# Moving the loop over overflow blocks of a mixture-of-experts layer from the end to behind the fifth step

## The reference, cut to what matters

```python
def run_block(args):
    toks, gts, ei = args
    xb = hf[toks]
    hb = jax.nn.silu(xb @ w1[ei]) * (xb @ w3[ei])      # 1024 -> 512
    return (hb @ w2[ei]) * gts[:, None]                # 512 -> 1024

ys = lax.map(run_block, (row_tok.reshape(-1, R), row_gate.reshape(-1, R), block_e))
return jax.ops.segment_sum(ys.reshape(P, D), row_tok, num_segments=T)
```

## Time and profile before

| what | value |
|---|---|
| median of 3 runs | 1550.96 us (1550.81 to 1551.97) |
| profiled execution | 1557.21 us |
| its span | 1555.1 us |
| PE busy | 1360.8 us (88%) |
| DVE busy | 605.8 us (39%) |
| ACT busy | 407.4 us (26%) |
| POOL busy | 82.0 us (5%) |
| DMA traffic | 326.68 MB, mean 210 GB/s |

### The profile page before, as it was taken

The page is one execution under the profiler, slowest core; times in us unless marked ns, Lnnn a source line. Parts: engine busy times, 40 slices in busy tenths (PEclk is TensorE's granted clock), DMA queues, the critical chain, the costliest instruction groups (busy, mean ns, idle before and its releaser), DMA issues.

```text
span 1555.1 us, 17299 instructions
## 1 busy us (share of the span) xinstructions
PE 1360.8 (88%) x6335; PEld 685.4 (44%) x6335; DVE 605.8 (39%) x1370; ACT 407.4 (26%) x894; POOL 82.0 (5%) x113
## 2 busy tenths in 40 slices
PE   4999999999997889988899927999999899899750
PEld 3644444555654444444455524444433343343320
DVE  2535457400345666666333363222222232222206
ACT  4243311114665655555133310000000000000005
POOL 0000000010003000000000001000000000000004
PEclk9999999999997999999999956999999999999885
DMA  9714135220006940000633354999999999999929
GB/s 338 156 41 142 67 118 213 83 80 0 1 1 159 278 165 1 0 1 0 262 118 109 121 202 145 385 394 406 393 402 400 416 397 400 407 397 411 403 83 306
DMA packets 109451, 326.68 MB, mean 210 GB/s; under 512 B 26796, under 2 KB 51000, under 8 KB 100792
## 3 DMA queue, kind: packets, MB, share of 16 engines
q1 hardware_dynamic: 96296, 295.67, 50.8%
q0 software_dynamic: 6288, 18.90, 3.8%
q10 hardware_dynamic: 6784, 11.02, 1.9%
HBM read 285.69 MB, written 42.49 MB: 211 GB/s over the span
## 4 chain that ended last, share of the span: by engine, by line
PE 31%; SPq 12%; DMA 8%; DVE 5%; issue 2%; ACT 2%; POOL 1%; ACTq 0%; DVEq 0%; POOLq 0%
SPq L652 9%; DMA arena<-expert_w 7%; PE ps L1472 7%; PE ps L1512 6%; PE ps L1562 4%; PE ps L1523 4%; PE ps L1378 2%; PE ps L1395 2%; PE ps L1415 2%; SPq L650 1%; ACT arena L1040 1%; POOL arena L840 1%; PE ps L1502 1%; SPq L699 1%; PE ps L1457 1%
## 5 line engine op out<-in xcount | busy, mean ns | idle before, releaser
L1231 PE MATMUL ps<-arena 128*128 128x512 f32 x512 | 222.0, 593 | 0.0
L1523 PE MATMUL ps<-arena 128*32 128x256 f32 (+1 forms) x1408 | 196.9, 498 | 26.4 <-DMA arena<-expert_w 24.1
L1562 PE MATMUL ps<-arena 128*32 128x256 f32 (+2 forms) x832 | 156.0, 509 | 4.7 <-issue 2.0
L1231 PEld LDWEIGHTS ps<-arena 128*128 128x128 f32 x512 | 96.6, 190 | 117.8 <-issue 117.7
L1242 PE MATMUL ps<-arena 128*128 128x512 f32 (+1 forms) x384 | 144.5, 535 | 1.4 <-DVE arena L1658 1.4
L1523 PEld LDWEIGHTS ps<-arena 128*32 128x32 f32 (+1 forms) x1408 | 73.6, 126 | 135.6 <-issue 118.4
L1512 PE MATMUL ps<-arena 128*128 128x512 f32 x256 | 117.8, 619 | 6.0 <-DVE arena L2069 6.0
L1472 PE MATMUL ps<-arena 128*128 128x512 f32 x256 | 112.7, 592 | 0.1
L1040 ACT ACTIVATE arena<-arena 128x640 f32<-128x640 f32 (+7 forms) x128 | 92.8, 726 | 61.3 <-DVE arena L1871 61.3
L1242 PEld LDWEIGHTS ps<-arena 128*128 128x128 f32 x384 | 72.8, 192 | 66.2 <-issue 57.3
L1395 PE MATMUL ps<-arena 128*128 128x128 f32 x528 | 80.5, 286 | 21.2 <-ACT arena L1040 9.2
(11 more groups left out here) (326 smaller groups left out, 1309.2 us busy)
## 6 DMA issues: line engine op xcount, KB each, us to landing
arena<-expert_w SPq DMA_DIRECT2D x99, 2048.0 KB, 33.9
arena<-ada_w SPq DMA_DIRECT2D x12, 2048.0 KB, 9.3
d_y<-arena SPq DMA_DIRECT2D x24, 512.0 KB, 6.4
arena<-x SPq DMA_DIRECT2D x16, 512.0 KB, 4.4
arena<-w_in SPq DMA_DIRECT2D x4, 2048.0 KB, 11.0
d_y<-arena ACTq DMA_DIRECT2D x40, 128.0 KB, 8.2
arena<-w_out SPq DMA_DIRECT2D x2, 2048.0 KB, 14.1
out<-arena SPq DMA_DIRECT2D x8, 512.0 KB, 2.6
```

The costliest lines, as they stand in the source:

```text
L1231: last = nc.tensor.matmul(b, w(k), hT[:, k, 512 * c:512 * c + 512], start=(k == 0), stop=(k == KT - 1))
L1523: last = nc.tensor.matmul(ps[width * j:width * j + width, 2 if width == 64 else 3, 0:span], xgT[s][:, k, lo:lo + width], w_up[slots[n]][:, ...
L1562: last = nc.tensor.matmul(dst, hid_T[s][:, at_:at_ + width], w_down[slot][:, k, span * j:span * j + span], start=(k == 0), stop=(k == 3))
```

## The change

The loop over overflow blocks stands behind step 4, in front of step 5. It has 4 rounds, each with six nested conditions and six blocks. It has its own semaphores (`over_...`), counted from 1, with one unit given by GpSimd at the start so that block 0 waits for nothing of its own. All blocks use the same buffers (`xg[0]`, `xgT[0]`, `act1[0]`, `hid_e[0]`, `yo[0]`) and the same three slots, 3, 4 and 1. In `USES` the three matrices of the overflow blocks stand as a step numbered 32 behind step 4, so the loads of steps 5 and later take other slots than before, and three of them (w2 of step 6, w1 and w3 of step 8) wait for the slots of the overflow block, which are free when VectorE has left the loop (`over_end`).

On TensorE, down of step 4 is done before the loop and no longer between the turn of step 6 and the turn of step 5's hidden rows. VectorE waits before the loop until step 4's result has been stored. GpSimd issues the gather of step 6 only after `over_end`, and TensorE goes on with step 5 after `over_end`.

```diff
+OVER_AT, OVER, PER = 4, NE, 6
 def weight_uses():
     uses = []
     for q in range(NE):
-        uses += [(1, q), (3, q)] + [(2, q - 1)] * (q > 0)
+        uses += [(1, q), (3, q)] + [(2, q - 1)] * (q > 0 and q != OVER_AT + 1)
+        if q == OVER_AT:
+            uses += [(2, q)] + [(n, OVER) for n in (1, 3, 2)]
     return uses + [(2, NE - 1)]
...
             for v in range(NS - 1, len(LOADS)):
                 n, q = LOADS[v]
+                if q == OVER and n == 1:
+                    for j in range(3):
+                        slot_free(USES[v + j - NS])
+                    sp_blocks = sp.value_load(block_tab[0:1, 28:29], min_val=NE, max_val=NB)
+                    with sp.Fori(0, (NB - NE) // PER) as i, ExitStack() as rest:
+                        for s in range(PER):
+                            rest.enter_context(sp.If(PER * i + NE + s < sp_blocks))
+                            load_over(i, s)
+                if q == OVER:
+                    continue
                 place = ORDER[q]
...
             for q in range(NE):
                 gather_rows(q)
+                if q == OVER_AT + 1:
+                    pool.wait_ge(xg_turned, OVER_AT + 1)
...
+                    pool.wait_ge(over_end, 1)
...
+            def over_block(i, s):                      # PE
+                b = PER * i + s
+                pe.wait_ge(over_xg_in, 16 * b + 16)
+                pe.wait_ge(over_xgT, b + 1)
+                for k in range(KT):
+                    last = nc.tensor.transpose(turned_at(k, P), xg[so][:, k::KT], ident)
...
             for q in range(NE):
                 static_up(q)
                 if q + 1 < NE:
                     f_turn(q + 1, (q + 1) % 2, STEP_ROWS[q + 1], (q + 1) // 2 + 1)
-                if q:
+                if q and q != OVER_AT + 1:
                     static_down(q - 1)
                 f_turn_hidden(q, q % 2, STEP_ROWS[q])
+                if q == OVER_AT:
+                    static_down(q)
+                    pe.wait_ge(xgT_ready, OVER_AT + 2)
+                    pe.wait_ge(yo_ready, OVER_AT + 1)
...
+                    pe.wait_ge(over_end, 1)
...
+                if q == OVER_AT:                       # DVE
+                    static_result(q)
+                    dve.wait_ge(y_stored[so], STORES[OVER_AT + 2])
+                    v_blocks = dve.value_load(block_tab[0:1, 28:29], min_val=NE, max_val=NB)
+                    with dve.Fori(0, (NB - NE) // PER) as i, ExitStack() as rest:
+                        for s in range(PER):
+                            rest.enter_context(dve.If(PER * i + NE + s < v_blocks))
+                            over_block(i, s)
+                    dve.drain().then_inc(over_end, 1)
```

More of the change, by code:

```diff
@@ L100 @@
     SLOT_OF[u] = v if v < NS else SLOT_OF[USES[v - NS]]
-    fills[SLOT_OF[u]] += 1
+    fills[SLOT_OF[u]] += u[1] != OVER
     FILLS[u] = 16 * fills[SLOT_OF[u]]
-OVER_SLOT = [[SLOT_OF[USES[len(LOADS) - NS + 3 * s + j]] for j in range(3)] for s in range(2)]
-OVER_FILLS = [[16 * fills[j] for j in slots] for slots in OVER_SLOT]
+OVER_SLOT = [SLOT_OF[(n, OVER)] for n in (1, 3, 2)]
 STORES = [0, 0]
@@ L408, in build @@
         out_turned, outs_read = sem("out_turned"), sem("outs_read")
-        wout_scaled, pool_e, router_in, xt_in = sem("wout_scaled"), sem("pool_e"), sem("router_in"), [sem(f"xt_in{i}") for i in range(2)]
+        wout_scaled = sem("wout_scaled")
         diag_ready = sem("diag_ready")
@@ L424, in build @@
         table_ready = sem("table_ready")
-        mod_out, mod_in = sem("mod_out"), sem("mod_in")
+        mod_hop = sem("mod_hop")
         stage_f, y_zeroed = sem("stage_f"), sem("y_zeroed")
-        idx_seen, store_seen = sem("idx_seen"), sem("store_seen")
+        idx_seen = sem("idx_seen")
+        over_w_in = [sem(f"over_w_in{j}") for j in range(3)]
+        over_xg_in, over_silu, over_hid, over_hid_turned, over_hidT, over_stored = (
+            sem("over_" + n) for n in ("xg_in", "silu", "hid", "hid_turned", "hidT", "stored"))
+        over_free = [sem("over_" + n) for n in ("turned", "xgT", "up_half", "up", "down", "yo", "yo_free")]
+        over_turned, over_xgT, over_up_half, over_up, over_down, over_yo, over_yo_free = over_free
+        over_end, over_landed = sem("over_end"), sem("over_landed")
+        so = OVER_AT % 2
         y_in = [sem(f"y_in{i}") for i in range(NT)]
@@ L661, in slot_free @@
                 n, q = use
-                if n == 1:
+                if q == OVER:
+                    sp.wait_ge(over_end, 1)
+                elif n == 1:
                     sp.wait_ge(up_half, q + 1)
@@ L874, in _ @@
                 b = ready(act, ("adam", i))
-                nc.scalar.copy(ada_sum[0][:, i, :], b).then_inc(ada_copied, 1)
-                act.wait_ge(ada_copied, i + 1)
-                act.sem_inc(bank_read[JOB[("adam", i)] % 8], 1)
+                read(nc.scalar.copy(ada_sum[0][:, i, :], b), ("adam", i))
             act.wait_ge(mod_ready, 1)
@@ L1125, in store @@
                                .then_inc(y_stored[s], 16)
+            def over_block(i, s):
+                b = PER * i + s
+                act.wait_ge(over_up_half, b + 2)
+                nc.scalar.activation(act1[so], ps[:, 2, :], ACT.Silu).then_inc(over_silu, 1)
+                act.wait_ge(over_yo, b + 2)
+                act.sem_inc(idx_seen, 1)
+                to = d_y[bass.ds(P * (b + NE), P), :]
+                for n in range(2):
+                    act.dma_start(to[64 * n:64 * n + 64, :], yo[so][64 * n:64 * n + 64, :]).then_inc(over_stored, 16)
+                act.wait_ge(over_stored, 32 * b + 32)
+                act.sem_inc(over_yo_free, 1)
@@ L1143, in _ @@
[L1143 to L1146, removed]
+                if q == OVER_AT:
+                    store(q, q % 2, STEP_ROWS[q], ORDER[q])
+                    act.wait_ge(table_ready, 1)
+                    a_blocks = act.value_load(block_tab[0:1, 28:29], min_val=NE, max_val=NB)
+                    with act.Fori(0, (NB - NE) // PER) as i, ExitStack() as rest:
+                        for s in range(PER):
+                            rest.enter_context(act.If(PER * i + NE + s < a_blocks))
+                            over_block(i, s)
+                    act.drain().then_inc(over_landed, 1)
@@ L1147, in _ @@
+            store(NE - 1, 1, STEP_ROWS[NE - 1], ORDER[NE - 1])
+            for s in range(2):
+                act.wait_ge(y_stored[s], STORES[NE + s])
+                act.sem_inc(idx_seen, 1)
             act.drain().then_inc(stage_f, 1)
@@ L1584, in _ @@
                     f_turn(q + 1, (q + 1) % 2, STEP_ROWS[q + 1], (q + 1) // 2 + 1)
-                if q:
+                if q and q != OVER_AT + 1:
                     static_down(q - 1)
                 f_turn_hidden(q, q % 2, STEP_ROWS[q])
-            static_down(NE - 1)
[L1590 to L1605, removed]
+                if q == OVER_AT:
+                    static_down(q)
+                    pe.wait_ge(xgT_ready, OVER_AT + 2)
+                    pe.wait_ge(yo_ready, OVER_AT + 1)
+                    pe.wait_ge(table_ready, 1)
+                    e_blocks = pe.value_load(block_tab[0:1, 28:29], min_val=NE, max_val=NB)
+                    with pe.Fori(0, (NB - NE) // PER) as i, ExitStack() as rest:
+                        for s in range(PER):
+                            rest.enter_context(pe.If(PER * i + NE + s < e_blocks))
+                            over_block(i, s)
+                    pe.wait_ge(over_end, 1)
+            static_down(NE - 1)
             pe.drain().then_inc(stage_f, 1)
@@ L2102, in static_result, with over_block @@
                 result(q, q % 2, STEP_ROWS[q], STORES[q] if q >= 2 else None)
-            dve.wait_ge(mod_in, 32)
+            def over_block(i, s):
+                b = PER * i + s
+                dve.wait_ge(over_turned, b + 2)
+                for k in range(KT):
+                    last = V.tensor_scalar(xgT[so][:, k, :], turned_at(k, P), scale_f[:, k:k + 1], shift_f[:, k:k + 1], ALU.mult, ALU.add)
+                last.then_inc(over_xgT, 1)
+                dve.wait_ge(over_silu, b + 1)
+                dve.wait_ge(over_up, b + 2)
+                V.tensor_tensor(hid_e[so], act1[so], ps[:, 3, :], ALU.mult).then_inc(over_hid, 1)
+                dve.wait_ge(over_hid_turned, b + 1)
+                V.tensor_copy(hid_T[so], ps[:, 4 + so, :]).then_inc(over_hidT, 1)
+                dve.wait_ge(over_down, b + 2)
+                dve.wait_ge(over_yo_free, b + 1)
+                V.tensor_copy(yo[so], ps[:, 6:8, :].rearrange("p a b -> p (a b)")).then_inc(over_yo, 1)
+            dve.wait_ge(mod_hop, 64)
             f_turned(0, 0, STEP_ROWS[0], True)
@@ L2109, in _ @@
                     f_turned(q + 1, (q + 1) % 2, STEP_ROWS[q + 1], q + 1 < 2)
[L2110 removed]
+                if q and q != OVER_AT + 1:
                     static_result(q - 1)
                 hidden_turned(q, q % 2, STEP_ROWS[q], q < 2)
[L2113 to L2128 removed]
```

(12 more changed lines are left out.)

136 lines of the change are left out of this document (67 added, 69 removed).

## The result

The changed kernel takes 1566.66 us (median of 4 runs, 1565.9 to 1569.21), the kernel before 1551.47 beside it (1550.81 to 1552.67). The ratio is 1.009 (95% interval 1.0062 to 1.0119): slower by 15.2 us. Forecast were 1565.7 us, with a range of 1556 to 1577. The profiled execution has a span of 1567.3 us, 12.2 more than before.

A forecast was written before the change was run, and what follows sets the result against it. DMA was taken as the harder of two nearly equal bounds. The load stream late by 49.5 us, less 34.7 us saved at the end, gave +14.8 us: median 1565.7 us, range 1556 to 1577.

The forecast's parts named there:

- What bounds: From 1043 to 1469 us: DMA engines full, TensorE idle 29 us; two nearly equal bounds, DMA the harder one.
- Down of step 4: TensorE before the moved loop: starts at 1031.9, takes 7.1 us, ends at 1039.0.
- The store wait: VectorE before the loop waits for both stores of step 4: 9.5 us, until 1050.8; bounds 3.1 and 10.9.
- The block: Overflow block behind step 4, from up to the copy's end: 29.4 us, ending at 1084.3.
- The rival of a clock at 1.2 GHz throughout: TensorE stays at 1.2 GHz through the overflow block: over_end 16.5 us later, 1582.2 us; chance 0.12.
- Leaving the loop: After the block's copy: four times 0.57 us plus 0.3 for the drain, giving over_end at 1086.8.
- The restart: Load stream after over_end: w2 of step 6 lands 8.6 us after issue, at 1095.4; stream late by 49.5 us.
- The queue in front of the held load: Loads before w2 of step 6: first lands at 1012.0, nine more at 6.2 us each by 1067.4.
- The tail: Behind the last static step: copy, four small stores and meeting remain, 7.7 us of 42.4; 34.7 us saved.
- From the sum to the median: Whole kernel: +14.8 us takes the profiled 1557.2 to 1572.0; profiled run 6.2 us above the median, so median 1565.7.
- TensorE's lag as a rival: At the restart behind step 4: TensorE's lag of 55.9 us counts, net +21.2 us, 1572.2 us; chance 0.15.
- The other side: Load stream during the block: not cut, net -8.2 us, 1542.8 us; chance 0.06, including over_end before 1070.

The follow-up runs named there:

- behind step 12: Changed kernel with the loop behind step 12 and VectorE's store wait moved to the copy that writes the same buffer: 1532.97 us, 0.988 of the kernel before.
- behind steps 16 and 20: Changed kernel with the loop behind step 16 or 20 and VectorE's store wait moved to the copy writing the same buffer: 1533.95 and 1539.06 us.
- behind step 16: Changed kernel with the loop behind step 16 instead of step 4, store wait still in front of the loop: 1549.82 us, 0.9979 of the kernel before.

## Why the prediction was right, step by step

- *What bounds* and the mechanism: right behind step 4, as the chain, the stretches with a DMA share of 0 and TensorE's waits for weights show: the cut stream sets the loss. The uncut stream behind step 12 takes it away.
- *Down of step 4*: forecast to end at 1039.0, ended at 1038.86.
- *The store wait*: 9.5 us were taken, 7.18 came. It lies within the bounds of the earlier trace rows; the median of the earlier trace rows, taken from the same two stores in the kernel before, where they were issued 4 us later, was too long by 2.3 us. The reason given for it, seven loads queued, was wrong: four were unfinished.
- *The block*: 29.4 us taken, 27.35 measured (1051.86 to 1079.21). Up took 16.66 us, as taken; down took 7.13 and not 8.85. TensorE had stood idle for 9 us, three times as long as before, and the clock cost no more for it: in both kernels the granted clock was 0.50, the 1.2 GHz level, in the first 4 us of this up, and 1.00 over its last 4. The rival of a clock at 1.2 GHz throughout did not come.
- *Leaving the loop*: 2.6 us taken, 1.9 seen between the end of the copy and TensorE's restart. But VectorE's sequencer goes on while the copy still runs: the first branch is at 1078.07 and the drain at 1081.02, so four rounds and the drain take 3.0 us, of which 1.1 lie beside the copy. The conditions of the last three rounds stand 0.7 us apart (first line below). In the kernel before, with two blocks to a round, eleven of them on VectorE stand 0.54 us apart (second line). So a round over six blocks costs VectorE 0.2 us more, and the 0.57 taken from ScalarE was too short. The Trainium skill (Advanced Engine Details and Errata, Control Flow Timing) had put the four rounds at 0.6 us by estimate; the trace does not agree.

```profile
L2188 DVEq COMPARE_BRANCH  x3: 56/56/56, 1079.2 to 1080.6; - x3
```

```profile
L2125 DVEq COMPARE_BRANCH  x11: 56/56/56, 1502.3 to 1507.7; - x11
```

- So `over_end` came at 1081.1, 5.7 us before the forecast. *The restart* ate this up: the first load took 14.3 us to land and not 8.6. The lag of the stream was 49.6 us, forecast 49.5. The sum was right there by luck: two errors of 5.7 us cancel. The lone load of the earlier trace rows had only one small gather beside it; here the block's two stores, two gathers and two more loads went out within 3 us of it. Without the block and its stores, but with both gathers and both loads, it took 11.5 us. What of the rest each of them costs was not tried.
- *The queue in front of the held load*: taken as nine loads at 6.2 us up to 1067.4; the block's first load landed at 1011.6 and the ninth after it at 1060.8, 5.5 us each. So DMA stood without a load for 6.6 us longer than forecast. This changed nothing in the sum, since the restart hangs on `over_end`, but "the stream isn't cut if it comes before about 1065" was too generous by that much.
- *The tail*: 7.7 us taken, 5.0 measured. The last of the four small stores landed in 2.9 us, where 5.1 was taken; before, the block's own weights were still on their way when they were issued.
- *From the sum to the median*: the profiles lie 12.2 us apart, forecast 14.8. The sum was 2.6 us too high, nearly all of it in the tail. The median was met within 1 us only because the new profiled execution lay 2.5 us above its median and not 6.2 as assumed. This too was luck.
- *TensorE's lag as a rival*: wrong behind step 4, where TensorE waits for weights after the restart; right behind steps 16 and 20.
- *The other side*: the stream uncut. It was priced at 1542.8 us for this place and did not come there. As a mechanism it was right. Where it did come, behind step 12, it was 10 us better than priced; the price has 9.2 us for the first gap, and the tail is 2.7 us shorter than taken.

## What to carry to other kernels

A drain in the middle of a kernel that is bound by loads costs what the transfers stand still, not what the compute engines stand still. Put it where the queue of issued loads is longer than the drain, and late enough that the queue is full, but early enough that the compute engine has slack left to make up its own lag: here step 12 met both, and from step 16 on the lag set the time. Put each wait in front of the instruction that needs it, not in front of the loop: a store's landing is not a fixed price, it took 3.1 to 18.3 us in these runs.

## What the runs showed of the hardware that was not expected

Stores are slowed by loads that another engine has queued, but not in step with their number. A whole result goes out in two stores of 256 KB. With no load under way both took 3.1 us to land (the block's in the kernel before), with two loads unfinished 7.2 and 9.1 (the block's behind step 12), with four 6.2 and 7.2 (step 4's), and with eight, at 1201.1 in the kernel before:

```profile
DMA to landing us min/median/max: 7.4/9.0/10.6
```

Stores that follow one another land later and later. In a row of six, issued from 1214.9 to 1217.7 in the kernel before, the first two took 7.5 and 9.5 us and the other four, though of 32 KB each, took

```profile
DMA to landing us min/median/max: 10.8/12.7/14.6
```

The 18.3 us behind step 16 are those of a store of 128 KB, the eighth within 5.3 us, with seven loads unfinished. And after a pause the DMA engines were busy but slow: just after the restart behind step 4 they showed a share of 1.05 at 281 GB/s, where full stretches move about 400:

```profile
1087.00:1095.00 8.00, 1.36 (x10) 1.17 (x10) 1.87 (x8) 0.00 (x0) 0.84 (x1) 0.77 1.05 281
```

A busy share near 1 is therefore no proof of full bandwidth. Why it is lower there is left open.
